# The projection for x, B and C of a state-space mixer: plain fp32 matmuls, or three fp32r passes of split operands

## The reference

```python
proj = h @ w_in[l]                      # h: 256 x 1024
p_ssd = proj[..., RWKV_COLS:RWKV_COLS + SSD_COLS]
z = p[..., :SSD_WIDTH]                                  # 2048 columns
xbc = p[..., SSD_WIDTH:SSD_WIDTH + SSD_CONV_CH]         # 3072 columns: x 2048, B 512, C 512
dt_raw = p[..., SSD_WIDTH + SSD_CONV_CH:]               # 32 columns: the step widths
xbc = jax.nn.silu(causal_dwconv(xbc, conv_w, conv_b))   # four taps along the tokens
dt = jax.nn.softplus(dt_raw.astype(f32) + dt_bias.astype(f32))
```

## Time and profile before

| | before |
|---|---|
| median of 3 runs, us | 2126.65 |
| the profiled execution, us | 2126.88 |
| its span in the trace, us | 2125.2 |
| TensorE busy | 82% |
| VectorE busy | 41% |
| ScalarE busy | 26% |
| TensorE clock granted, mean | 0.908 |

### The profile page before, as it was taken

The page is one execution under the profiler, slowest core; times in us unless marked ns, Lnnn a source line. Parts: engine busy times, 40 slices in busy tenths (PEclk is TensorE's granted clock), DMA queues, the critical chain, the costliest instruction groups (busy, mean ns, idle before and its releaser), DMA issues. The chain is left out here.

```text
span 2125.2 us, 31311 instructions
## 1 busy us (share of the span) xinstructions
PE 1742.2 (82%) x13367; PEld 1262.7 (59%) x13367; DVE 870.3 (41%) x1308; ACT 550.6 (26%) x777; POOL 50.4 (2%) x51
## 2 busy tenths in 40 slices
PE   3786899877678999885787988879749999898886
PEld 1585799754456998785686875567534433333332
DVE  1444555422545544776566455555531111111111
ACT  1323444212444443432102013344211110110001
POOL 0000000000000000011300000000000000000000
PEclk9797999987669999997898998989859999999998
DMA  6311745232006554340001342434269999999993
GB/s 233 134 65 40 277 168 206 80 123 83 1 1 239 208 186 158 120 159 11 3 4 42 119 151 72 176 120 138 91 247 376 394 394 393 392 393 394 390 390 149
DMA packets 173532, 388.84 MB, mean 183 GB/s; under 512 B 10327, under 2 KB 20787, under 8 KB 172639
## 3 DMA queue, kind: packets, MB, share of 16 engines
q1 hardware_dynamic: 169166, 378.19, 48.7%
q0 software_dynamic: 2560, 8.39, 1.1%
q10 hardware_dynamic: 1680, 0.43, 0.1%
HBM read 385.79 MB, written 1.20 MB: 182 GB/s over the span
## 5 line engine op out<-in xcount | busy, mean ns | idle before, releaser
L2650 DVE TENSOR_TENSOR moe_hidT<-moe_silu,ps 128x256 f32<-128x256 f32 x32 | 13.5, 422 | 433.6 <-ACT moe_silu L2609 433.6
L1195 DVE TENSOR_TENSOR mlp_w_lo<-weight_slots,mlp_w_hi 128x2048 fp32r<-128x2048 f32 x64 | 143.8, 2289 | 59.1 <-ACT mlp_w_hi L1165 59.1
L2573 PE MATMUL ps<-moe_slots,moe_h 128*64 128x512 f32 x512 | 148.0, 619 | 20.0 <-DMA moe_slots<-in_w_exp_up 15.7
L2573 PE MATMUL ps<-weight_slots,moe_h 128*64 128x512 f32 x512 | 146.5, 612 | 20.1 <-DMA weight_slots<-in_w_exp_up 9.9
L136 PE MATMUL ps<-mlp_h_hi,mlp_w_hi 128*128 128x256 f32 x512 | 145.0, 283 | 2.4 <-DVE mlp_w_lo L1195 2.4
L138 PE MATMUL ps<-mlp_h_hi,mlp_w_lo 128*128 128x256 f32 x512 | 144.9, 283 | 0.0
L137 PE MATMUL ps<-mlp_h_lo,mlp_w_hi 128*128 128x256 f32 x512 | 144.9, 283 | 0.0
L1165 ACT ACTIVATE mlp_w_hi<-weight_slots 128x2048 fp32r<-128x2048 f32 x64 | 119.6, 1908 | 58.4 <-PE ps L138 47.9
L2573 PEld LDWEIGHTS ps<-moe_slots,moe_h 128*64 128x64 f32 x512 | 48.7, 142 | 97.8 <-issue 92.1
L2573 PEld LDWEIGHTS ps<-weight_slots,moe_h 128*64 128x64 f32 x512 | 48.4, 140 | 94.9 <-issue 93.7
L136 PEld LDWEIGHTS ps<-mlp_h_hi,mlp_w_hi 128*128 128x128 f32 x512 | 98.2, 192 | 4.6 <-DVE mlp_w_lo L1195 4.0
(11 more groups left out here) (583 smaller groups left out, 3715.7 us busy)
## 6 DMA issues: line engine op xcount, KB each, us to landing
weight_slots<-in_w_in SPq DMA_DIRECT2D x20, 2048.0 KB, 7.7
weight_slots<-in_w_up SPq DMA_DIRECT2D x16, 2048.0 KB, 8.9
weight_slots<-in_w_down SPq DMA_DIRECT2D x16, 2048.0 KB, 7.8
weight_slots<-in_w_exp_gate SPq DMA_DIRECT2D x16, 2048.0 KB, 20.0
weight_slots<-in_w_exp_up SPq DMA_DIRECT2D x16, 2048.0 KB, 22.8
moe_slots<-in_w_exp_up SPq DMA_DIRECT2D x16, 2048.0 KB, 23.0
moe_slots<-in_w_exp_down SPq DMA_DIRECT2D x16, 2048.0 KB, 20.2
moe_slots<-in_w_exp_gate SPq DMA_DIRECT2D x16, 2048.0 KB, 20.2
```

What stands on the lines that cost most here:

```text
L1195: dve.tensor_tensor(piece_slot(w_split[1], jj), raw_piece(jj), piece_slot(w_split[0], jj).bitcast(F32), ALU.subtract).then_inc(w_lo, 1)
L2573: mm = pe.matmul(ps[side(kind), 0, :], h_sel[:, k, :], w[kind][:, k, :], start=(k == 0), stop=(k == KD - 1))
L2650: dve.tensor_tensor(hid_T[:, :, :], opened_sb[:, :, :], turned_up, ALU.mult)\
```

## The change

The stage xbc becomes a `split_stage` with depth 2 for its 24 chunks; the step widths stay plain fp32 matmuls, through a new kind of product ("plain") that reads the unsplit weights in their slot. The slots of x, B and C are then free for the next load when the last piece is split, the small one when its product is done. The four split buffers need room: `ssd_x` is allocated after the stage, and `ssd_xT` at the right end of SBUF. Everything else stands as it was; lines behind the change have other numbers (L485 is L489 after, L2043 and L2047 are L2039 and L2043).

```diff
-        def sb(name, shape, dt=F32, on=None):
+        def sb(name, shape, dt=F32, on=None, side=None):
...
-            return (on or ctx).enter_context(nc.sbuf_tensor(name, shape, dt))
+            return (on or ctx).enter_context(nc.sbuf_tensor(name, shape, dt, side=side) if side
+                                              else nc.sbuf_tensor(name, shape, dt))
...
-                                _, w = piece(2 * n + half)
+                                raw, w = piece(2 * n + half)
...
-                                        if kind == "feature":
+                                        if kind == "plain":
+                                            mm = pe.matmul(bank(job)[0:width, 0:S], raw[:, k, c0:c0 + width],
+                                                           src[:, c, :], start=begin, stop=end)
+                                        elif kind == "feature":
...
-                        for n, (u, _, _) in enumerate(units):
-                            stream.done[u] = (w_lo, 2 * (n + 1) + 1)
+                        for n, (u, _, products) in enumerate(units):
+                            read_raw = products[0][1] == "plain"
+                            stream.done[u] = (full, products[0][0] + 1) if read_raw else (w_lo, 2 * (n + 1) + 1)
...
-                xs = sb("ssd_x", [P, NT, SW], on=on)
...
-                    xT = sb("ssd_xT", [P, SW // P, S], on=on2)
+                    xT = sb("ssd_xT", [P, SW // P, S], on=on2, side="right")
...
-                    def produce(pe, j, bank):
-                        if j == nx + nb:
-                            stream.arrived(pe, ud)
-                            return feature_chunk(pe, ud, 0, SH, bank[0:SH, 0:S])
-                        if j % 4 == 0:
-                            stream.arrived(pe, u0 + j // 4)
-                        return feature_chunk(pe, u0 + j // 4, (j % 4) * P, P, bank[:, 0:S])
...
-                    stage("xbc", nx + nb + 1, produce, consume, on_vector=lambda j: True,
-                          uses={**{u0 + i: 4 * i + 3 for i in range(6)}, ud: nx + nb})
+                    split_stage("xbc", feature_products(u0, nx + nb) +
+                                [(ud, 0, [(nx + nb, "plain", 0, SH, None, True, True)])],
+                                consume, hT, depth=2, on_vector=lambda j: True)
+                    xs = sb("ssd_x", [P, NT, SW], on=on)
```

## The result

The changed kernel takes 2134.06 us (median of six, 2133.17 to 2138.0), the kernel before 2126.78 beside it: ratio 1.0035, 95% interval 1.0022 to 1.0048, so it is slower by 4.7 to 10.2 us, 7.3 by the medians. The forecast was 2131.0, 4.3 us slower, with a range of 2127.5 to 2134.5; the way and the range held, the size was too small.

A forecast was written before the change was run, and what follows sets the result against it. TensorE bounds the stage today and VectorE would after the change; order +1.1, start clock +1.5, later clock 1.3 + 0.4 make +4.3 us on 2126.88, less 0.23 to the median: 2131.0. Range 2127.5 to 2134.5.

The forecast's parts named there:

- rival B: Stage xbc: each TensorE wait costs a stretch at half clock, +6.0 us in all, 2132.7 us; chance 20%.
- TensorE's work: Stage xbc: 82.9 us of plain matmuls replaced by 69.1 us of fp32r ones at 0.120 each; TensorE alone gains 13.8.
- VectorE's work: Stage xbc: 2.00 us a chunk plus 2.2 a low half make 12.4 us a unit against TensorE's 11.5; VectorE becomes bound.
- the signs of being right: Stage xbc: VectorE busy about 79 us, longest TensorE wait about 3 us before the third unit, stage 90 to 93 us.
- The order step by step: Stage xbc laid out at full clock: TensorE waits 3.1 us behind VectorE's consuming; ends at 88.3 against 87.2, +1.1 us.
- 0.9, 2.2, 0.9 and 0.2: Stage xbc: TensorE's waits in us for the low halves of pieces 6, 8, 10 and 12.
- The clock at the start: Start of stage xbc: TensorE pauses about 3.8 us, then runs 3.4 us at the lower clock, +1.5 us.
- The clock behind the later waits: Stage xbc: the 3.1 us wait probably brings half clock, the 2.2 one every second time; +1.3 + 0.4 us.
- A: Rival, stage xbc: VectorE keeps up and TensorE runs through; 82.2 against 87.2 us, 5.0 faster, 2121.7; chance 7%.
- C: Rival, stage xbc: the clock holds or only the start costs; +1.1 to +2.6 us, 2128 to 2129; chance 9%.
- D: Rival, stage xbc: three fp32r passes cost three quarters of plain, 0.108 us a matmul; +1.0 us, 2127.7; chance 4%.
- What costs nothing: Weight loads, slots, the placement of ssd_x and ssd_xT: no cost; the stage's difference reaches the end one to one.

The follow-up runs named there:

- after_one_tap: Changed kernel with three of VectorE's four convolution taps per chunk left out: stage 78.1 us, ratio to the kernel before 0.9952.
- woven_act_tap: Changed kernel with ScalarE's and VectorE's work reordered and each chunk's first tap moved to ScalarE: stage 78.4 us, ratio to the kernel before 0.9957.
- after: The changed kernel itself, run beside the kernel before: stage 94.4 us, ratio 1.0035.
- filled: Changed kernel with useless TensorE matmuls in its three longest waits (6 at the start, 6 and 5 later): stage 89.3 us, ratio to the kernel before 0.9989.
- best: woven_act_tap plus six useless TensorE matmuls at the stage's start: stage 76.9 us, 2117.36 us, ratio to the kernel before 0.9952.
- act_tap: Changed kernel with each chunk's first convolution tap moved from VectorE to ScalarE: stage 83.0 us, ratio to the kernel before 0.9975.
- woven: Changed kernel, same instructions, with splits written between pairs of chunks on ScalarE and VectorE: stage 83.7 us, ratio to the kernel before 0.9980.
- place: Kernel before with only the new placement of ssd_xT and ssd_x, projection still plain fp32: stage 87.5 us, ratio to the kernel before 1.0000.
- filled_start: Changed kernel with only the 6 useless TensorE matmuls at the stage's start: stage 91.8 us, ratio to the kernel before 1.0019.

## Why the prediction was right, and where its size was off

The mechanism was right: VectorE's written order makes TensorE wait, and the clock falls behind some of the waits. The size was not: 4.3 us were forecast, and the measured 4.7 to 10.2 leave that just outside. That the time still lies in the range, 0.4 us below its upper end, owes something to luck, since that end was drawn for rival B, whose mechanism did not come.

**TensorE's work.** 0.120 us a matmul held (the rows at 1207.74, 1207.86 and 1207.98), and so did the 69.1 us: after_one_tap and woven_act_tap, in which they set the end, came within 0.4 of sums made with it. By the four passes that the Trainium skill ("FP8 and Floating Point Precision", TensorE Precision Notes) gives for true fp32, one pass would be 0.431 / 4 = 0.108, an estimate. The trace disagrees for an fp32r matmul: 0.120.

**VectorE's work.** 2.00 us a chunk and 2.20 for a low half that follows at once (1209.02 to 1213.42 is 4.40 for two) held to a few hundredths. VectorE was busy 75.9 us where the signs of being right had about 79, and the stage, counted from ScalarE's first instruction as there, lasted 94.1 where they had 90 to 93. That VectorE becomes the bound is shown from both sides: less load (one tap), and the same load in another order.

**The order step by step.** "PE waits 3.1 us" before the third unit: 3.10 in the trace, at the place named. "0.9, 2.2, 0.9 and 0.2" behind it did not come so in after: the trace has none, 3.09, none and 1.09. At full clock they did come. In filled the waits behind the third unit's are 0.67, then the 2.3 us that the useless matmuls fill, then 0.66 and 0.19, and the low halves of pieces 4, 6, 8, 10 and 12 are ready at 29.2, 41.7, 55.6, 68.1 and 80.0 us where the forecast had 29.0, 41.4, 55.2, 67.6 and 79.3. So the order was right, and small drifts add up to 0.7: the stage is 89.3, +1.8, where the sum said +1.1.

The forecast laid this order out at full clock and added the clock's price behind it, so it missed how a slow stretch changes the waits after it. The first one makes TensorE late, which swallows its wait of 0.9. But TensorE then frees its buffer late too, so ScalarE's next high half and VectorE's low half behind it come late: VectorE waits 2.83 us for that high half in after (1226.57), 1.44 in filled (1222.31). All of VectorE's work behind it moves by 1.4, and the wait of 2.2 becomes 3.09, as long as the first, which the forecast had taken to bring a fall; to one of 2.2 it gave a fall every second time.

```profile
1226.57 2.29 DVE L489 TENSOR_TENSOR xbc_w_lo<-weight_slots,xbc_w_hi 128x2048 fp32r<-128x2048 f32 x1 [2.83 <-ACT xbc_w_hi L466]
1222.31 2.29 DVE L511 TENSOR_TENSOR xbc_w_lo<-weight_slots,xbc_w_hi 128x2048 fp32r<-128x2048 f32 x1 [1.44 <-ACT xbc_w_hi L488]
```

**The clock at the start.** +1.5 forecast, 1.5 measured (woven_act_tap against best), though in the stage where TensorE sets the end.

**The clock behind the later waits.** This is the term that was mis-sized. Forecast 1.3 + 0.4, with the second stretch taken as one in two and 3.4 us long. Both came, and the second lasted 6.1 us in the profiled run. after less filled is 5.1; without the start's 1.5 that leaves 3.6 in place of 1.7: 1.4 for the first, as forecast, and 2.2 for the second, priced at 0.4. Why the second lasted longer than the first is open. Of the whole miss in the stage, 6.9 against 4.3, this makes 1.9 and the order 0.7.

**Rivals.** A (VectorE keeps up) fell: it needs under 11.5 us a unit, and the runs that bring it there, act_tap and after_one_tap, are the ones that are fast. B (every wait costs clock, 20%) came nearer in size, +6.0 against +6.9 in the stage, but not in its mechanism: two of the waits that it priced didn't exist, the 1.09 before the step widths and the waits under 0.8 in filled, woven and act_tap brought no fall, and the second wait of 3.1 cost more than it had. C and D are excluded, by the three stretches at 0.50 and by the pitch.

**What costs nothing** held: place is 1.0000, and the parts behind the stage agree within 0.8 us.

## What to carry to other kernels

When a faster form of matmul moves work to another engine, sum that engine's work for a round of the loop, then write down its order and see what each split stands behind: here the sum alone (12.4 against 11.5 us a unit) would have cost far less than the order did, and the same instructions in another order turn +6.9 us into -3.8. Waits of 2 to 3 us on TensorE can cost more than their length, since the clock may fall behind each (it did behind all four of 3.1 us in after and filled_start); lay the order out with the slow stretches in it, as they move the next waits. And price a consumer that is hidden today before it has to share its engine: three taps that cost nothing before cost 16 us after.

## What the runs showed of the hardware

Two waits of the same length, 3.10 and 3.09 us, in the same kernel were followed by 3.1 and by 6.1 us of matmuls at half clock. In filled_start, nearly the same program, both waits of 3.09 were followed by 3.4; there TensorE first went on at full clock, for about 1.3 and 0.7 us. Waits of 0.2 to 0.8 us (woven, act_tap) were never followed by a fall. Six matmuls of no use, 2.8 us of TensorE's time, kept the granted clock at 1.00 in a wait of 3.8 us (filled, filled_start, best) and in one of 3.1 (filled). ScalarE takes about 0.55 us for a 128x256 activation from PSUM with a scale and a bias for each partition, as much as VectorE's tap of 0.54, so which of the two has room decides. ScalarE's row of it, from the time line of best:

```profile
1203.82 0.55 ACT L2076 ACTIVATE ssd_xT<-ps,cols 128x256 f32<-128x256 f32 x1
```
